# Two transformer blocks in one kernel: a modulation tile loaded earlier, the token norm by halves, and four squares behind another weight split

## The reference

```python
# first block (hgrn2 mixer, then a conv FFN); 256 latent tokens and 256 context tokens
m_l = silu(c) @ w_ada + b_ada            # 6 vectors of 1024: shift, scale, gate, twice
m_c = silu(c_ctx) @ w_ada + b_ada
hl = rmsnorm(x, g) * (1 + sc1) + sh1     # latent tokens
hc = rmsnorm(ctx, g) * (1 + csc1) + csh1 # context tokens
lat = x + g1 * hgrn2_mixer(hc, hl, w_in, ...)
lat = lat + g2 * conv_ffn(rmsnorm(lat, g') * (1 + sc2) + sh2)
x = rmsnorm(lat, final_g)
# second block (retention and sliding window attention, then an MLP)
x = x + rmsnorm(merged @ w_out, post_mix_norm)
h = rmsnorm(x, pre_mlp_norm)
u = square(relu(h @ w_up))               # 4096 wide
x = x + rmsnorm(u @ w_down, post_mlp_norm)
```

## Time and profile before

| | |
|---|---|
| median of three runs | 878.05 us (877.91 to 878.32) |
| profiled execution | 878.34 us |
| its span | 876.3 us |
| TensorE busy | 865.5 us, 99% |
| VectorE busy | 645.5 us, 74% |
| ScalarE busy | 484.7 us, 55% |
| loads | 160.9 MB |
| granted TensorE clock | 1.00 of full speed in all slices |

### The profile page before, as it was taken

One profiled execution on the slowest core, in us unless ns is written; L12 is line 12 of the kernel. 1 busy time (PEld: TensorE's weight loads), 2 busy tenths in 40 slices (PEclk: granted clock), 3 DMA queues, 4 the chain that ended last, 5 costly groups with the idle time before them and its releaser, 6 DMA issues.

```text
span 876.3 us, 17163 instructions
## 1 busy us (share of the span) xinstructions
PE 865.5 (99%) x6416; PEld 789.6 (90%) x6416; DVE 645.5 (74%) x1095; ACT 484.7 (55%) x763; POOL 0.2 (0%) x4
## 2 busy tenths in 40 slices
PE   8999999999999999999999999999999999999997
PEld 3688888888899999999999999999998889999996
DVE  3893899999997787876668979865477765555555
ACT  4443677777765655555557555454554654444443
POOL 0000000000000000000000000000000000000000
PEclk9999999999999999999999999999999999999999
DMA  9974444444446557556563644445465465555551
GB/s 343 409 283 154 144 148 146 144 143 144 164 150 236 190 209 249 174 190 200 164 203 129 206 145 147 153 164 174 144 215 171 143 196 192 189 191 184 180 186 48
DMA packets 45585, 160.91 MB, mean 184 GB/s; under 512 B 5216, under 2 KB 6624, under 8 KB 45408
## 3 DMA queue, kind: packets, MB, share of 16 engines
q1 hardware_dynamic: 43632, 156.43, 51.6%
q10 hardware_dynamic: 1904, 3.81, 1.2%
HBM read 159.16 MB, written 1.05 MB: 183 GB/s over the span
## 4 chain that ended last, share of the span: by engine, by line
PE 93%; ACT 2%; DVE 2%; DMA 1%; SPq 1%; issue 1%; DVEq 0%; ACTq 0%
PE bank L429 22%; PE bank L431 22%; PE bank L430 22%; PE bank L483 4%; PE bank L485 4%; PE bank L484 4%; PE bank L1203 2%; PE bank L1206 2%; PE bank L1204 2%; DMA arena<-in_ada 1%; PE bank L451 1%; PE bank L1294 1%; PE bank L1312 1%; PE bank L1174 1%; PE bank L456 1%
## 5 line engine op out<-in xcount | busy, mean ns | idle before, releaser
L423 DVE TENSOR_TENSOR w_lo<-raw,w_hi 128x1024 fp32r<-128x1024 f32 x244 | 295.1, 1222 | 116.8 <-ACT w_hi L416 116.3
L429 PE MATMUL bank<-h_hi,w_hi 128*128 128x256 f32 (+1 forms) x1216 | 363.8, 299 | 0.0
L431 PE MATMUL bank<-h_hi,w_lo 128*128 128x256 f32 (+1 forms) x1216 | 357.7, 294 | 0.0
L430 PE MATMUL bank<-h_lo,w_hi 128*128 128x256 f32 (+1 forms) x1216 | 356.2, 293 | 0.0
L416 ACT ACTIVATE w_hi<-raw 128x1024 fp32r<-128x1024 f32 x244 | 252.6, 1050 | 97.0 <-PE bank L431 75.7
L429 PEld LDWEIGHTS bank<-h_hi,w_hi 128*128 128x128 f32 x1216 | 228.4, 188 | 9.6 <-issue 1.9
L430 PEld LDWEIGHTS bank<-h_lo,w_hi 128*128 128x128 f32 x1216 | 230.1, 189 | 6.5
L431 PEld LDWEIGHTS bank<-h_hi,w_lo 128*128 128x128 f32 x1216 | 228.2, 188 | 5.8
L429 PE MATMUL bank<-y_hi,w_hi 128*128 128x256 f32 x304 | 87.0, 286 | 0.1
L431 PE MATMUL bank<-y_hi,w_lo 128*128 128x256 f32 x304 | 85.8, 282 | 0.0
L430 PE MATMUL bank<-y_lo,w_hi 128*128 128x256 f32 x304 | 85.4, 281 | 0.0
(11 more groups left out here) (263 smaller groups left out, 1066.0 us busy)
## 6 DMA issues: line engine op xcount, KB each, us to landing
raw<-in_stream SPq DMA_DIRECT2D x244, 512.0 KB, 3.3
arena<-in_ada SPq DMA_DIRECT2D x40, 512.0 KB, 6.4
xres<-in_ada SPq DMA_DIRECT2D x8, 512.0 KB, 3.2
tok<-in_tok SPq DMA_DIRECT2D x3, 512.0 KB, 8.1
con<-in_con ACTq DMA_DIRECT2D x1, 1472.0 KB, 6.2
xres<-in_tok ACTq DMA_DIRECT2D x1, 1024.0 KB, 9.8
out<-arena SPq DMA_DIRECT2D x4, 256.0 KB, 2.0
tok<-in_tok SPq DMA_DIRECT2D x2, 256.0 KB, 8.6
```

The costliest lines, as they stand in the source:

```text
L423: dve.tensor_tensor(w_lo[c.slot][:, :], raw[c.slot][:, :], w_hi[c.slot][:, :].bitcast(F32), ALU.subtract).then_inc(S("split_lo"), 1)
L429: pe.matmul(dst, hi_w, a_hi, start=start, stop=False, skip_group_check=True)
L430: pe.matmul(dst, hi_w, a_lo, start=False, stop=False, skip_group_check=True)
L431: return pe.matmul(dst, lo_w, a_hi, start=False, stop=stop, skip_group_check=True)
```

## The change

Three places are changed, none of which changes what is computed.

1. SyncE issues modulation tile 3 behind token piece 2 instead of behind piece 4.
2. The token norm goes by halves. The log and the exp are each split into an instruction for the 256 latent tokens and one for the 256 context tokens, and ScalarE modulates half 0 of tile 0 before it takes the exp of half 1. ScalarE copies the sums of quarter 0 before it squares the last piece. VectorE waits for `rstd` by halves and makes the low part of half 0 before it norms half 1. On TensorE, `ada(3)` moves ahead of `token_sum(2)`, `turn_rows(0)` ahead of `token_sum(3)`, `ada(5)` behind the first two value groups, together with `ada(6)`; `ada(7)` goes behind the fourth group, and `turn_rows(1)` behind the sixth.
3. In the second MLP, at j = 2, ScalarE makes the high part of the next chunk before the four squares instead of after them.

```diff
--- before.py
+++ after.py
@@ -719,9 +719,9 @@
             load_ada(2)
             load_tokens(1)
             load_tokens(2)
+            load_ada(3)
             load_tokens(3)
             load_tokens(4)
-            load_ada(3)
             load_one(0)
             sp.dma_start(par[:, :], par_in).then_inc(S("par_in"), 16)
             for q in range(1, QUARTERS):
@@ -803,27 +803,49 @@
                 act.wait_ge(S("ada_summed"), q + 1)
                 act.activation(mod_rows[q], psum[4 + q][:, :], ACT.Copy).then_inc(S("mod_rows"), 1)
 
+            def modulate_half(k, half):
+
+                at, gain, shift = (k * TC, gain_l, mod) if half == 0 else (k * TC + T, gain_c, mod_c)
+                act.wait_ge(S("mod_first"), k // 2 + 1)
+                act.wait_ge(S("tok_normed"), 2 * k + half + 1)
+                act.activation(h_hi[:, at:at + T], tok[:, at:at + T], ACT.Identity, scale=gain[:, k:k + 1],
+                               bias=shift[:, k:k + 1]).then_inc(S("h_hi"), 1)
+
             def modulate(k):
 
-                act.wait_ge(S("mod_first"), k // 2 + 1)
-                for half, (at, gain, shift) in enumerate(((k * TC, gain_l, mod), (k * TC + T, gain_c, mod_c))):
-                    act.wait_ge(S("tok_normed"), 2 * k + half + 1)
-                    x = tok[:, at:at + T]
-                    act.activation(h_hi[:, at:at + T], x, ACT.Identity, scale=gain[:, k:k + 1],
-                                   bias=shift[:, k:k + 1]).then_inc(S("h_hi"), 1)
-
-            for n in range(5):
+                for half in range(2):
+                    modulate_half(k, half)
+
+            def square_piece(n):
+
                 x = slice(PIECES[n] * TC, PIECES[n + 1] * TC)
                 act.wait_ge(S(f"tok_in{n}"), 16)
                 act.activation(wide[:, x], tok[:, x], ACT.Square).then_inc(S("tok_squares"), 1)
+
+            def log_sum(half):
+
+                x = slice(half * T, (half + 1) * T)
+                act.activation(rstd[:, x], psum[1][:, x], ACT.Ln, scale=1.0 / D, bias=eps).then_inc(S("tok_rstd"), 1)
+
+            def root(half):
+
+                x = rstd[:, half * T:(half + 1) * T]
+                act.wait_ge(S("tok_rstd"), 2 * half + 1)
+                act.activation(x, x, ACT.Exp, scale=-0.5).then_inc(S("tok_rstd"), 1)
+
+            for n in range(4):
+                square_piece(n)
             copy_rows(0)
+            square_piece(4)
             hi(act, Chunk(0))
             act.wait_ge(S("tok_summed"), 4)
             act.wait_ge(S("eps"), 1)
-            act.activation(rstd, psum[1][:, :], ACT.Ln, scale=1.0 / D, bias=eps).then_inc(S("tok_rstd"), 1)
-            act.wait_ge(S("tok_rstd"), 1)
-            act.activation(rstd, rstd, ACT.Exp, scale=-0.5).then_inc(S("tok_rstd"), 1)
-            modulate(0)
+            log_sum(0)
+            root(0)
+            log_sum(1)
+            modulate_half(0, 0)
+            root(1)
+            modulate_half(0, 1)
             modulate(1)
             copy_rows(1)
             hi(act, Chunk(1))
@@ -1124,10 +1146,10 @@
                 if j >= 1:
                     hi(act, Chunk(mlp_first(j), AHEAD))
                     mlp_tile(j - 1, (j - 1) % 2, (j - 1) % 4, mlp_first(j - 1) + 1, j >= 3)
+                if j >= 2:
+                    hi(act, Chunk(mlp_first(j), 1 + AHEAD))
                 if j == 2:
                     square_x()
-                if j >= 2:
-                    hi(act, Chunk(mlp_first(j), 1 + AHEAD))
             with act.Fori(0, (JM - MLP_PEEL) // 4 - 1) as i:
                 for u in range(4):
                     hi(act, Chunk(mlp_first(MLP_PEEL), 2 * u + AHEAD, i, 8))
@@ -1216,14 +1238,14 @@
             token_sum(0)
             warm(FILL[1])
             token_sum(1)
+            ada(3, 4)
             token_sum(2)
-            ada(3, 4)
-            token_sum(3)
             pe.wait_ge(S("con_in"), 16)
             turn_rows(0)
-            ada(4, 6)
+            token_sum(3)
+            ada(4, 5)
             warm(FILL[2])
-            values(0, {(0, 1): lambda: ada(6, 8), (0, 3): lambda: turn_rows(1)})
+            values(0, {(0, 1): lambda: ada(5, 7), (0, 3): lambda: ada(7, 8), (1, 1): lambda: turn_rows(1)})
             values(1, {(0, 1): lambda: ada(8, 12), (1, 0): lambda: turn_rows(2)})
             values(2, {(0, 1): lambda: ada(12, 16), (1, 0): lambda: turn_rows(3)})
             for j in range(3, KT):
@@ -1672,8 +1694,8 @@
 
             def norm_half(k, half):
 
-                if k == half == 0:
-                    dve.wait_ge(S("tok_rstd"), 2)
+                if k == 0:
+                    dve.wait_ge(S("tok_rstd"), 2 * half + 2)
                 x = tok[:, k * TC + half * T:k * TC + (half + 1) * T]
                 dve.tensor_tensor(x, x, rstd[:, half * T:(half + 1) * T], ALU.mult).then_inc(S("tok_normed"), 1)
 
@@ -1716,11 +1738,11 @@
             quarter(0)
             lo(dve, Chunk(0))
             norm_half(0, 0)
-            norm_half(0, 1)
             shift_half(0, 0)
             low_half(0, 0)
+            norm_half(0, 1)
+            norm_half(1, 0)
             shift_half(0, 1)
-            norm_half(1, 0)
             low_half(0, 1)
             norm_half(1, 1)
             shift_tokens(1)
```

## The result

The changed kernel takes 879.64 us (median of 19 runs, 879.12 to 880.62) against 878.06 for the kernel before (19 runs): 1.58 us more, a ratio of 1.0016 with a 95% interval of 1.0010 to 1.0023. The interval leaves out 1, so the changed kernel is slower, though by less than the 1.8 us (0.2%) that the prediction takes as what a measurement can tell from no change; the forecast was 879.3. The profiled execution took 879.72 us with a span of 877.9, 1.6 us longer than the span of before.

What follows compares the result with a forecast made beforehand. TensorE was taken as the bound, busy 99% of the span, so only its start and its waits count. Head +2.0 and MLP -0.7 gave +1.3 us on 878.05, forecast 879.3, with 878.8 to 880.0 about it.

Steps and rivals of the forecast that it cites:

- The new start: Start of the kernel: earlier tile 3 and the halved norm bring the first value matmul from 20.97 to 20.4, gaining 0.57 us.
- The order on TensorE: In values(0): ada(7) ends 1.99 us later, TensorE waits 1.05 at values(1), which starts 1.54 later.
- S': Forecast moment of the first value matmul in the changed kernel: 20.4 us, with bounds 20.2 and 21.0.
- rival A: At values(1): the chain is shorter than read and TensorE does not wait; +0.5, time 877.8 us; chance 0.12.
- The rest at `turn_rows(2)`: Transposes of quarter 2: no slack there, VectorE is 1.99 us late, so TensorE loses the rest of the 1.99.
- the head: Everything from the start through turn_rows(2): TensorE ends up 2.0 us later than before.
- The squares: Second MLP: moving the split ahead of four squares removes a 0.71 us wait at mlp_down, with nothing replacing it; -0.7 us.
- The sum: Whole kernel: 2.0 - 0.7 = +1.3 us, giving a forecast median of 879.3; chance 0.60.
- B: Before the first value matmul: the moved ada pass costs nothing, TensorE's idle time there being larger; 876.8 us; chance 0.06.
- D: Start: the norm is no earlier, the last token piece and sums eating the halving's gain; +1.85, 879.9 us; chance 0.10.
- C: Second MLP: the gain does not come because the split behind the squares becomes the late one; +2.0, 880.05 us; chance 0.09.

Runs made afterwards that it cites:

- late_tile_only: Kernel before with only TensorE's order inside values(0) edited: ada(6) behind the second group, ada(7) behind the fourth, turn_rows(1) behind the sixth; 880.55 us against 878.18.
- split_first: The change with the high part of chunk 1 ahead of copy_rows(1) on ScalarE instead of behind it; 879.01 us against 878.47 for the kernel before.
- order_back: The change with ada(4, 6), ada(6, 8) and turn_rows(1) in their old places on TensorE, filler matmuls kept; 877.50 us against 878.47 for the kernel before.
- copy_ahead: The change with copy_rows(2) ahead of the softmax exp on ScalarE instead of behind it; 879.17 us against 878.29 for the kernel before.
- change_again: The change run once more, unaltered; 879.63 us against 878.47 for the kernel before.
- three_tiles: The change with ada(5), ada(6) and ada(7) together behind the second value group and turn_rows(1) behind the fourth; 878.12 us against 878.18 for the kernel before.
- order_back_no_fill: The change with TensorE's old places for modulation tiles and transposes, and without the two filler matmuls ahead of the first value matmul; 877.47 us against 878.47 before.
- squares_only: Kernel before with the four squares behind the split in the second MLP as the only edit; 877.76 us against 878.18.

## Why the prediction held, step by step

**The new start: right.** Forecast 20.4 for the first value matmul, measured 20.22 with loads 0.24 us earlier. From the first square it is 11.93, where the forecast amounts to 11.87. The last sum (17.04 forecast, 16.84 measured), the log (18.14 and 18.00), the exp (18.64 and 18.51) and the norm (19.13 and 18.96) came in the order and at the distances worked out. The prediction credits halving with the gain; it did not see that the old norm stood behind VectorE's low part of chunk 0 and not behind the exp, and that the earlier `quarter(0)` had to clear this first.

**The order on TensorE: right.** Forecast for the end of `ada(7)` was S' + 5.14, measured 25.36 - 20.22 = 5.14. `quarter(1)` followed 2.84 after it (forecast 2.86), and the first matmul of `values(1)` 4.27 (forecast 4.29). The wait was 0.94 (forecast 1.05). late_tile_only and split_first show that this chain, in this order, is what TensorE waited for, and order_back that the time returns with the old order. In this reading the extra pass is part of the loss, too: without the wait, 1.15 us of work less the 0.5 gained at the start would remain, about 0.65 us, where rival A has 0.5.

**The rest at `turn_rows(2)`: right in kind.** I had the head at 2.0 behind it. It is 1.72 on the profile's clock and 1.9 to 2.0 counted from the first square; copy_ahead takes back 0.3 of it by moving one copy.

**The squares: right.** 0.71 forecast, 0.70 measured, and no wait took its place.

**The sum: 1.3 forecast, 1.58 measured.** Between the two profiled executions the difference is 1.72 in the head, -0.70 at the squares and 0.56 by the loop's pace, 1.6 in all. The head's 1.72 would be 1.97 had the loads started alike, so by the traces the kernels differ by 1.8, or by 1.6 with the head and the pace (0.37) of change_again. The forecast had the first two terms right and no term for the pace. The medians can't tell the two sums apart: they give 1.58 (0.9 to 2.0) and 1.16 (0.2 to 1.8), and 1.3 lies in both intervals. That the forecast came so near with one term missing is in part luck.

**The rivals.** A and B assumed that TensorE does not wait at `values(1)`; it does. D assumed that the norm does not start earlier; it starts 0.5 earlier. C, that the squares' gain is lost to a late split, fell: that split was in time. Most of its effect on the sum came in another way, by the loop's pace.

**What stays open: the pace.** Nine profiles take 158.48 us for the 28 steps, three take 158.85 (change_again, three_tiles, order_back) and one 159.04 (the change). All kernels that lack the new start or the moved squares are among the nine, but so are split_first, copy_ahead and order_back_no_fill, which have both. In the two that I compared at the same step, ScalarE and VectorE do the same work at the same distances to within 0.02 us, and TensorE doesn't wait; the 24 matmuls of 256 columns and the 12 of 512 follow each other by a fraction of a nanosecond more on average. The two profiles of the kernel of squares_only have the same pace; the two of the change are both slow, but not equally, so the kernel alone does not set it. That each kept to its side speaks for a part of the kernel in it, but two pairs are few. What sets it was not found.

**What else stays open.** No run has the moved load without the halved norm or the halved norm without the load, so what each is worth at the start is only read from the rows.

## What to carry to other kernels

When a step is moved within a list of in-order queues, follow the last step that waits for its result, not the step itself: here one small matmul group moved back by 2 us held a copy, behind the copy an unrelated weight split, behind that a bias for the next product, and it is that product that waited. A gain at the start of a chain is worth only what the chains behind it let through (of 0.44 us at the first value matmul nothing was left in order_back_no_fill), and part of it may hang on a single copy that stands behind something else's wait. And where a small edit fills a wait that no other work depended on, as the split ahead of four squares did, it can be read off the trace to a hundredth of a microsecond.

## What the runs showed that I had not expected

Matmuls with 32 output columns cost by whole passes here. A modulation tile fills two of the four column groups: one tile holds TensorE 0.98 us (24.38 to 25.36 in the change), two hold it 1.00, three 1.84 and four 1.85. In this kernel tiles should be grouped by two.

The start of the loads varies from one execution to the next: the first token piece released its square between 8.00 and 9.34 us in 13 profiles, while the third square followed the first by 3.83 to 4.06 us in twelve of them and by 4.43 in split_first. A difference of half a microsecond between two profiles of a kernel like this says nothing until it is counted from such a landing.

TensorE's pace in the MLP loop differed by up to 0.35% (5.66 and 5.68 us for a step) at a granted clock of 1.00 in both, and over 28 steps that was 0.56 us in the change's profile, a third of the whole measured difference, and 0.37 in its repeat.
